# Experts of a routed layer in plain float32: two experts side by side in one block of 128 slots, a ring of 16 weight loads, results stored by token

## The chip, the cores and the metric

The kernel runs on one core of one Trainium2 chip, in one launch. The metric is the device time of that core in microseconds. The core has TensorE (PE: matmuls, with its weight loads shown as PEld), VectorE (DVE), ScalarE (ACT), GpSimd (POOL), a queue engine SyncE (SP) that issues most DMAs, and 16 DMA engines between the chip's main memory and the core's SBUF. The result of a matmul lands in PSUM. Each engine runs its own instruction list in order and waits for the others on semaphores.

## What is computed

Two layers (DEPTH 2) of a backbone on 256 context tokens and 512 latent tokens, width 1024, all in float32. Each layer has a token mixer (latent attention, neighbourhood attention, Fourier mixing, gates) and then routed experts. Layer 0 runs the experts for 768 tokens, layer 1 for the 512 latent ones. The change touches the experts alone:

```python
N_EXPERTS, TOP_K, D_MODEL, D_EXPERT = 32, 2, 1024, 512
def hier_moe(h, ...):
    p_grp = softmax(h @ w_rg + b_rg);  p_top, g_idx = top_k(p_grp, 1)        # 4 groups of 8
    e_in = (h @ w_re + b_re)[group g_idx];  l_top, e_loc = top_k(e_in, 2)
    w_tok = p_top * softmax(l_top);  e_ids = g_idx * 8 + e_loc
    for each token and each of its two experts e, weight w:
        out[token] += w * ((silu(x @ w_gate[e]) * (x @ w_up[e])) @ w_down[e])
```

w_gate and w_up are 1024x512 for each expert and w_down is 512x1024, 2 MiB each, 6.3 MB an expert and 201 MB a layer. With the reference's inputs the router gives these loads: in layer 0 the three fullest experts have 147, 139 and 99 tokens, the ninth fullest of experts 4 to 31 has 54, and experts 0 to 3 have 24, 35, 46 and 27. In layer 1 the fullest has 101, the ninth fullest of experts 4 to 31 has 45, and experts 0 to 3 have at most 15.

## The kernel before, in words

It is written for the five engines by hand: a function per engine, each a Python list of instructions, with semaphores between them (`then_inc`, `wait_ge`). Both layers are unrolled. Most tiles lie in one large SBUF tensor called `arena`, so a profile row reads `arena` for nearly all of them; `round` is the same memory seen as float32r, `slot`, `vbank` and `abank` are PSUM tiles, `xb` and the rest are slices of arena.

**Router.** For each tile of 128 tokens TensorE transposes the normalised rows (L807) and multiplies them with the router's weights (L813). SP stores the rows to `h_rows` in memory (L2247). VectorE then finds the group and the two experts of every token (L1375 to L1409). TensorE counts how many earlier tokens chose the same expert (L848, L851, L854), and from that a one-hot product gives for each expert the list of its tokens (L862, `ids`). `dest` says for each token and choice in which slot of `y_slots` its result will stand.

**Expert stage.** Each of the 32 experts has one block of 128 slots, in order of its number. POOL gathers the 128 rows of a block from `h_rows` by `ids` (L1998, two buffers `xb`). TensorE transposes them (XT, L890), does gate and up into `slot[0]`, transposes the product (AT, L918) and does down into `slot[1]` (L899 for all three). Weights come in units of 1 MiB, six for an expert (gate, gate, up, up, down, down). SP loads a unit into one of six raw buffers (L2269), in pieces of 2 KB, as soon as the unit that lay there has been split. ScalarE rounds it to float32r (`upper`, L1789), VectorE forms the difference (`lower`, L1458), both into a ring of four. Each product is then three products of float32r parts:

```python
for m, (st_, w) in enumerate(((ph, whi[n0 % RING]), (ph, wlo[n0 % RING]), (pl, whi[n0 % RING]))):
    last = pe.matmul(out_ap, st_, w[:, k, :], ...)        # L897 to L899
```

ScalarE copies the result of a block (L1811) and issues its store to `y_slots` (L1813), all 128 rows of it. One turn of the hardware loop does two experts (12 units). The down part of a block runs one block late, after gate and up of the next one.

**Start of the stage.** SP issues four units after the last row store and after the output projection's last matmul. A barrier of all five engines follows (L355); then the other units, the first transposes and the writing of the slot lists (L2013) begin.

**Extra blocks.** An expert with over 128 tokens gets more blocks, decided at run time: `ctl` holds their number and their experts, and each engine runs `extra_block` under a branch, 11 of them (NX), in plain float32 (L962, L969, L974, L980), with weights loaded whole (L2303 to L2309). Two of them run in layer 0 and none in layer 1. SP issues list and weights of the first one when all units have been split; POOL gathers its rows (L2028), ACT stores its result (L1862).

**End of the stage.** After a barrier POOL gathers for each token tile the two result rows by `dest` (L2044), TensorE mixes them with the token's two weights (L1000), and VectorE adds, normalises and goes on to the next layer or to the output. Slots of extra blocks that nobody writes are zeroed once at the start (L2127).

## Time and profile before

| | us |
|---|---|
| time, median of 3 runs | 3227.08 (3225.95 to 3227.56) |
| time of the profiled execution | 3230.56 |
| its span, first to last instruction | 3228.8 |
| TensorE busy | 2897.7 (90%) |
| VectorE busy | 1861.6 (58%) |
| ScalarE busy | 1401.7 (43%) |
| GpSimd busy | 420.4 (13%) |
| first expert matmul to the end of the last, layer 0 | 1049.9 to 1655.6 |
| the same, layer 1 | 2562.1 to 3166.8 |
| moved by DMA | 665.18 MB, mean 206 GB/s |

The profile is of one execution. Its span is 1.8 us shorter than that execution's own time, and that time lies 3.5 us above the median. Busy time of an engine is the union of its instructions; a busy engine need not be the one that the others wait for, which the chain of waits tells: it goes back from the last instruction to what released it. PE is matmuls, PEld the loads of the stationary operand that run beside them. A plain float32 matmul leaves two records, a float32r one leaves one. The clock is TensorE's granted clock as a share of 2.4 GHz. A row of a line in a helper function stands for all its callers.

### The profile page before, as it was taken

Reading aid. Unit: us, or ns where it says so; the run is one execution under the profiler, and the core shown is the slowest. Engines: PE = TensorE matmul, PEld = TensorE weight load, DVE = VectorE, ACT = ScalarE, POOL = GpSimd, SP = SyncE. Lnnn points to the kernel's source line nnn. Section 1 sums busy time; section 2 is a strip of 40 time slices with the busy share of each in tenths; the row PEclk is TensorE's granted clock in tenths of the full one; section 3 lists DMA queues with packets and bytes.
Section 4 is the critical chain, followed back from the end, with each engine's and each line's share of the span. In section 5 each row is a group of like instructions: output and inputs, shape, how many; then the busy total and the mean of one; then the engine's idle time right before and its main releaser. Section 6 shows DMA issues by size and latency. Waiting matters only on the chain.

```text
span 3228.8 us, 37959 instructions
## 1 busy us (share of the span) xinstructions
PE 2897.7 (90%) x13895; PEld 2091.6 (65%) x13895; DVE 1861.6 (58%) x2243; ACT 1401.7 (43%) x1710; POOL 420.4 (13%) x403
## 2 busy tenths in 40 slices
PE   5999898999995999999986699898999599999994
PEld 3655566788844787777752355466885488777772
DVE  3223566422247788888834413456334688888884
ACT  2200346422101677777730210346320377777770
POOL 1220000001112211111002310000011201111102
PEclk7999999999996999999988799999999699999997
DMA  9740002222143999999983550003333599999993
GB/s 303 245 156 26 6 1 36 69 69 59 46 139 113 349 393 392 392 393 392 392 318 150 172 164 26 6 2 75 97 104 120 182 379 392 392 392 392 392 392 122
DMA packets 400599, 665.18 MB, mean 206 GB/s; under 512 B 63744, under 2 KB 139920, under 8 KB 400096
## 3 DMA queue, kind: packets, MB, share of 16 engines
q1 hardware_dynamic: 365154, 541.75, 48.7%
q0 software_dynamic: 25824, 87.22, 7.6%
q10 hardware_dynamic: 9504, 34.61, 2.6%
q8 instruction: 79, 1.29, 0.2%
q14 instruction: 38, 0.31, 0.0%
HBM read 612.95 MB, written 53.39 MB: 206 GB/s over the span
## 4 chain that ended last, share of the span: by engine, by line
PE 52%; DMA 23%; DVE 11%; ACT 9%; issue 3%; SPq 1%; DVEq 0%; POOL 0%; PEldq 0%; ACTq 0%; POOLq 0%
DMA arena<-in_w_gate_e 22%; PE abank L771 11%; PE abank L559 7%; PE slot L899 7%; PE vbank L771 5%; PE slot L827 4%; DVE round L1458 4%; ACT round L1789 3%; PE vbank L612 3%; PE vbank L597 2%; PE vbank L696 2%; DVE nmx L1204 1%; PE vbank L528 1%; ACT arena L1603 1%; PE abank L584 1%
## 5 line engine op out<-in xcount | busy, mean ns | idle before, releaser
L899 PE MATMUL slot<-round,round 128*128 128x512 f32 x4608 | 1107.5, 397 | 62.3 <-DVE round L1466 57.5
L899 PEld LDWEIGHTS slot<-round,round 128*128 128x128 f32 x4608 | 860.2, 190 | 259.6 <-issue 54.3
L1458 DVE TENSOR_TENSOR round<-arena,round 128x2048 fp32r<-128x2048 f32 x384 | 872.5, 2287 | 161.0 <-ACT round L1789 160.7
L1789 ACT CAST round<-arena 128x2048 fp32r<-128x2048 f32 x384 | 734.5, 1915 | 327.0 <-DMA arena<-in_w_down_e 92.2
L771 PE MATMUL abank<-round,round 128*128 128x512 f32 (+1 forms) x1152 | 324.3, 360 | 8.3 <-DVE round L1279 8.3
L1998 POOL DMA_INDIRECT arena<-h_rows,ids x64 | 141.7, 2214 | 970.5 <-PE vbank L890 919.1
L771 PEld LDWEIGHTS abank<-round,round 128*128 128x128 f32 x1152 | 207.5, 190 | 43.2 <-issue 8.7
L559 PE MATMUL abank<-arena 128*128 128x512 f32 (+1 forms) x640 | 229.1, 517 | 3.3 <-ACT arena L1603 3.3
L1305 DVE TENSOR_TENSOR arena<-vbank,arena 128x512 f32<-128x512 f32 x72 | 43.4, 602 | 310.6 <-PE vbank L771 310.6
L771 PE MATMUL abank<-hT_low,round 128*128 128x512 f32 (+1 forms) x576 | 207.3, 360 | 0.0
L559 PEld LDWEIGHTS abank<-arena 128*128 128x128 f32 x640 | 121.9, 193 | 114.8 <-issue 102.9
L771 PE MATMUL vbank<-round,round 128*128 128x512 f32 (+1 forms) x864 | 178.2, 355 | 0.0
L1761 ACT ACTIVATE arena<-abank,bT 128x512 f32<-128x512 f32 x72 | 44.5, 618 | 290.5 <-PE abank L771 290.5
L771 PEld LDWEIGHTS vbank<-round,round 128*128 128x128 f32 x864 | 144.3, 189 | 24.3
L827 PE MATMUL slot<-arena 128*128 128x512 f32 x320 | 138.4, 593 | 3.4 <-POOL arena L1983 3.4
L1072 DVE SCALAR_TENSOR_TENSOR arena<-vbank,arena 2x512 f32<-2x512 f32 x20 | 13.6, 679 | 215.3 <-PE vbank L528 215.3
L1983 POOL TENSOR_TENSOR arena<-arena 128x512 f32<-128x512 f32 (+1 forms) x48 | 53.1, 1106 | 609.6 <-DVE arena L1305 609.6
L1616 ACT ACTIVATE arena<-abank,bT 128x512 f32<-128x512 f32 (+3 forms) x48 | 25.3, 543 | 231.8 <-PE abank L559 231.8
L771 PEld LDWEIGHTS abank<-hT_low,round 128*128 128x128 f32 x576 | 109.5, 190 | 17.0
L1279 DVE TENSOR_TENSOR round<-arena,round 128x1536 fp32r<-128x1536 f32 x48 | 89.2, 1858 | 52.6 <-ACT round L1728 52.6
L827 PEld LDWEIGHTS slot<-arena 128*128 128x128 f32 x320 | 60.5, 190 | 78.7 <-issue 74.6
L1662 ACT ACTIVATE arena<-slot,nmx 128x768 f32<-128x768 f32 (+1 forms) x80 | 65.2, 815 | 100.3 <-DVE nmx L1204 100.0
(248 smaller groups left out, 3402.2 us busy)
## 6 DMA issues: line engine op xcount, KB each, us to landing
arena<-in_w_gate_e SPq DMA_DIRECT2D x128, 1024.0 KB, 14.1
arena<-in_w_up_e SPq DMA_DIRECT2D x128, 1024.0 KB, 12.5
arena<-in_w_down_e SPq DMA_DIRECT2D x128, 1024.0 KB, 14.2
arena<-in_w_ada POOLq DMA_DIRECT2D x80, 512.0 KB, 5.0
y_slots<-arena ACTq DMA_DIRECT2D x66, 512.0 KB, 6.4
arena<-in_w_in SPq DMA_DIRECT2D x48, 512.0 KB, 4.2
arena<-in_w_in SPq DMA_DIRECT2D x8, 2048.0 KB, 12.6
arena<-in_w_ada SPq DMA_DIRECT2D x4, 2048.0 KB, 15.2
```

The costliest lines, as they stand in the source:

```text
L559: last = pe.matmul(ps[:, 0:nn], w[:, k, m * P:(m + 1) * P], hT[:, k, o:o + nn], start=(k == 0), stop=(k == KD - 1))
L597: last = pe.matmul(ps[:, 0:384], hT[:, k, t * P:(t + 1) * P], w[:, k, 0:384], start=(k == 0), stop=(k == KD - 1))
L612: last = pe.matmul(ps[:, 0:512], hT[:, k, t * P:(t + 1) * P], w[:, k, :], start=(k == 0), stop=(k == KD - 1))
L696: last = pe.matmul(ps[64 * e:64 * e + 64, 0:P], v[:, k, h * 64:(h + 1) * 64], PT[(i + e) % 4][:, k, :], start=(k == 0), stop=(k == kt - 1))
L771: last = pe.matmul(ps[:, 0:n], x, y, start=(k == 0 and q == 0), stop=(k == len(terms) - 1 and q == 2))
L827: last = pe.matmul(s[:, half * 512:(half + 1) * 512], mT[:, k, t * P:(t + 1) * P], w, start=(k == 0), stop=(k == KD - 1))
L899: last = pe.matmul(out_ap, st_, w[:, k, :], start=(first and k == 0 and m == 0), stop=(final and k == 3 and m == 2))
L1279: dve.tensor_tensor(glo[u % 2], graw[u % GRAW], ghi[u % 2].bitcast(F32), ALU.subtract).then_inc(glo_ready, 1)
L1458: dve.tensor_tensor(wlo[n0 % RING][:, :, :], raw[n0 % RAW][:, :, :], whi[n0 % RING][:, :, :].bitcast(F32), ALU.subtract).then_inc(lo_ready, 1)
L1662: act.activation(PR[i % 2][:, 0:nk], slot[(ib + i) % 2][:, 0:nk], ACT.Exp, bias=nmx[:, k:k + 1], scale=1.0, accum_out=rsum[:, k:k + 1]).th ...
L1789: act.copy(whi[n0 % RING][:, :, :], raw[n0 % RAW][:, :, :]).then_inc(hi_ready, 1)
L1998: pool.indirect_dma_start(out=xb[i % 2], out_offset=None, in_=h_d[:, :], in_offset=bass.IndirectOffsetOnAxis(ap=ids[:, i:i + 1], axis=0)). ...
```

## The change

- **Plain float32.** The splits into float32r parts go, on ScalarE and VectorE, for weights, rows and the middle. TensorE multiplies the loaded units themselves, one product where there were three.
- **Blocks of two experts.** A layer has 20 blocks of 128 slots instead of 32 (NB). Experts 0 to 3 stand in two fixed pairs. The other 28 are ranked by their number of tokens: the eight fullest have a block alone, the next 20 are paired. In a pair, slots 0 to 63 belong to one expert and 64 to 127 to the other: a product has a stationary operand of 128x64 and writes half of the partitions of a PSUM tile, and the two experts' products alternate. The order is the two fixed pairs, two ranked pairs, then eight times a single block and a pair.
- **Ranking.** VectorE and TensorE work out rank, block, half and capacity (128 alone, 64 in a pair) of each expert. The two fixed pairs' lists (`ids`, first two columns) are made first, the ranked ones while blocks 0 and 1 run. SP reads the ranked expert numbers from `eord` (a value load before the first unit of each) and addresses the weights with them.
- **Loads.** The ring has 16 units of 1 MiB, released by the matmuls themselves (`unit_used`). A unit's rows are dealt so that each partition reads 8 KB in one piece: four rows of gate or up, two whole rows of half the down matrix. xT and aT are taken in the matching order by a strided view. Four units are issued ahead of the row stores, ten behind them, two after the router's last transposes.
- **Rows and results by token.** `h_rows` holds every row twice (SP stores each tile twice), for first and second choice. A list names rows 0 to 1535, or 4096 for an empty slot, which a bounds check leaves out of gather and store. Results go by the same list to `y_rows` (POOL, an indirect store per block), so at the end SP loads them as plain tiles. `y_slots`, its zeroing and `dest` for whole blocks go.
- **Extra blocks** hold only what exceeds 128 or 64 slots; 15 may be needed. SP issues list and weights of the first one after the last unit has been used. POOL does gather, store and the wait for its landing, one block after the other.
- **Barriers** within and around the stage go, except those between the layers' phases elsewhere.

```diff
-RAW, RING = 6, 4
-UNITS = 6 * NE
+FIXED, HOT = 4, 8
+RANKED = NE - FIXED
+NB = FIXED // 2 + HOT + (RANKED - HOT) // 2
+NX = (2 * TOK - HOT * (P // 2 + 1)) // (P // 2)
+RAW = 16
...
+    order = pairs + cold[:spare]
+    for h, c in zip(hot, cold[spare:]):
+        order += [h, c]
...
+                def gate_or_up(i, part):
...
+                    for half in range(2):
+                        tiles = weights(i, part, half)
+                        for j in range(4):
+                            for at, w in tiles:
+                                last = pe.matmul(to[at, :], xT[i % 2][:, 4 * half + j, at], w[:, j, :],
+                                                 start=(half == 0 and j == 0), stop=(half == 1 and j == 3))
+                        release(last, i, part, half)
+                        if part == "gate" and half == 0 and i:
+                            middle_turned(i - 1)
...
+                rows_turned(0)
+                for i in range(NB):
+                    gate_or_up(i, "gate")
+                    gate_or_up(i, "up")
+                    if i + 1 < NB:
+                        rows_turned(i + 1)
+                    if i == 0:
+                        ranked_ids()
+                    else:
+                        down(i - 1)
+                middle_turned(NB - 1)
+                down(NB - 1)
...
-                    dst = raw[n0 % RAW]
-                        src = wdf[bass.ds(i * FE + (L * NE - 1) * FE, FE), (c - 4) * 512:(c - 3) * 512]
-                    sp.dma_start(dst, src.rearrange("(k p) f -> p k f", p=P)).then_inc(raw_in[n0 % RAW], 16)
+                        sp.dma_start(raw[n % RAW], src.rearrange("(p j) f -> p j f", j=4)).then_inc(raw_in[n % RAW], 16)
...
                 def extra_block(j, b, it):
                     with pool.If(count > j):
...
+                        pool.wait_ge(X["dve"], j * 3 + 3)
+                        pool.sem_inc(X["go"], 1)
+                        pool.indirect_dma_start(
+                            out=y_d[:, :], out_offset=bass.IndirectOffsetOnAxis(ap=idx_x[:, b:b + 1], axis=0),
+                            in_=yb[0], in_offset=None,
+                            bounds_check=2 * TOK - 1, oob_is_err=False).then_inc(X["y"], 16)
+                        pool.wait_ge(X["y"], j * 16 + 16)
+                        pool.sem_inc(X["y_out"], 1)
...
+                        if isinstance(j, int):
+                            sp.wait_ge(unit_used, mark["unit_used", L, len(units) - 1])
+                        else:
+                            sp.wait_ge(X["y_out"], j * 1)
```

What the change does to the instruction lists, at three places. Names with numbers (`round_4_62`) are single float32r views, the shape is the output's, `x16` counts instructions alike.

TensorE inside the first gate part of layer 0, before: two slices k of one unit.

```order
L899 MATMUL slot<-round_4_62,round_8_70 128x512
L899 MATMUL slot<-round_4_66,round_8_70 128x512
L899 MATMUL slot<-round_4_62,round_8_72 128x512
L899 MATMUL slot<-round_4_63,round_8_70 128x512
L899 MATMUL slot<-round_4_67,round_8_70 128x512
L899 MATMUL slot<-round_4_63,round_8_72 128x512
```

TensorE after, around the first block of a single expert (L993 gate and up, L1010 down, L966 and L976 transposes):

```order
L993 MATMUL slot<-arena 64x512 x24
L966 MATMUL vbank<-cst,arena 128x128 x4
L966 MATMUL abank<-cst,arena 128x128 x4
L1010 MATMUL slot<-arena 64x512 x16
L993 MATMUL slot<-arena 128x512 x4
L976 MATMUL abank<-cst,arena 128x128 x4
L993 MATMUL slot<-arena 128x512 x12
```

Where 24 products of three kinds stood for a unit pair's worth of weights there are 8 for one expert and 16 of 64 partitions for two; the down part of the pair before stands between the transposes and the next gate part.

SP at the start of layer 0's stage, before, from the last router bias on:

```order
L2069 DMA arena<-in_b_re 128x32
L2247 DMA h_rows<-arena 128x1024 [waits hrow_ready] x6
L2269 DMA arena<-in_w_gate_e 128x4x512 [waits groups_done]
L2269 DMA arena<-in_w_gate_e 128x4x512
L2269 DMA arena<-in_w_up_e 128x4x512 x2
L2269 DMA arena<-in_w_gate_e 128x4x512 [waits h_out1,h_out0,phase_act,phase_pool,phase_dve,phase_pe]
L2269 DMA arena<-in_w_gate_e 128x4x512
L2269 DMA arena<-in_w_up_e 128x4x512 [waits lo_ready] x2
```

SP after, from the last row store on (the four units of w_gate_e that now stand ahead of the twelve row stores are left out):

```order
L2316 DMA h_rows<-arena 128x1024 [waits hrow_ready]
L2316 DMA h_rows<-arena 128x1024
L2309 DMA arena<-in_w_up_e 128x2048 [waits groups_done]
L2309 DMA arena<-in_w_up_e 128x2048 x3
L2309 DMA arena<-in_w_gate_e 128x2048 x4
L2309 DMA arena<-in_w_up_e 128x2048 x2
L2309 DMA arena<-in_w_up_e 128x2048 [waits h_out1,h_out0,groups_done]
L2309 DMA arena<-in_w_up_e 128x2048
L2304 DMA arena<-in_w_down_e 128x2048 [waits unit_used,expert_order]
```

Ten units stand behind the row stores with no wait for another engine's phase, where four stood, and the first wait for a used unit comes at the 17th.

POOL at the end of layer 0's stage, before:

```order
L1998 DMA arena<-h_rows,ids 128x1024 [waits xt_done] x30
L2019 TENSOR_LOAD ctl
L2019 ISA x2
L2022 COMPARE_AND_BRANCH [waits xt_done]
L2028 DMA arena<-h_rows,idx_x 128x1024 [waits x0_ids0]
L2022 UNCONDITIONAL_BRANCH
L2036 MEMSET arena 128x128 [waits phase_act,phase_sp,phase_dve,phase_pe]
```

POOL after, from the last result stores to the first extra block:

```order
L2034 DMA y_rows<-arena,ids 1536x1024 [waits y_ready] x5
L2065 TENSOR_LOAD ctl [waits y_stored0,y_stored1,vec_taken]
L2065 ISA x2
L2067 MEMSET arena 128x128
L2070 COMPARE_AND_BRANCH
L2076 DMA arena<-h_rows,idx_x 128x1024 [waits x0_ids0]
L2082 DMA y_rows<-arena,idx_x 1536x1024 [waits x0_dve]
L2070 UNCONDITIONAL_BRANCH [waits x0_y]
```

The first extra gather now stands behind the wait for all result stores, and each extra block has its store, and the wait for it, ahead of the next block's gather.

## Rows read from the trace of the kernel before

**Rows 1.** The page's line of GB/s, 40 slices of 80.7 us each.

```profile
GB/s 303 245 156 26 6 1 36 69 69 59 46 139 113 349 393 392 392 393 392 392 318 150 172 164 26 6 2 75 97 104 120 182 379 392 392 392 392 392 392 122
```

**Rows 2.** Stretches: us, busy of PE, PEld, DVE, ACT, POOL, clock, DMA, GB/s.

```profile
1000.00:1050.00 50.00, 23.06 (x113) 21.10 (x111) 33.21 (x77) 12.21 (x13) 10.35 (x8) 0.50 0.48 167
...
1042.00:1656.00 614.00, 582.73 (x2688) 474.62 (x2688) 522.78 (x350) 453.07 (x351) 89.34 (x43) 0.98 1.02 377
2554.00:3167.00 613.00, 581.02 (x2688) 474.68 (x2688) 522.73 (x351) 452.94 (x351) 76.41 (x38) 0.98 1.01 374
```

**Rows 3.** Chain of waits, layer 0: start us, us, engine, tile, line, count.

```profile
1138.82 14.06 DMA arena<-in_w_gate_e
...
1648.20 7.36 PE slot L899 x24
...
1667.56 16.31 PE slot L969 x32
...
1699.85 14.02 PE slot L969 x32
...
1717.32 10.16 PE slot L980 x16
...
1744.37 5.14 PE slot L1000 x8
```

**Rows 4.** DMA queues from 1200 to 1400 us: packets, MB, share of 16 engines.

```profile
q1 hardware_dynamic: 33858, 67.25, 90.7%
q10 hardware_dynamic: 1584, 5.77, 7.1%
q0 software_dynamic: 1506, 5.45, 7.0%
```

**Rows 5.** DMA packets from 2457 to 2465 us, before the expert stage of layer 1.

```profile
DMA packets 894, 3.26 MB, mean 407 GB/s; under 512 B 102, under 2 KB 102, under 8 KB 893
```

**Rows 6.** Chain of waits, dense stretches of TensorE (the columns of rows 3).

```profile
893.96 55.20 PE slot L827 x128
...
1083.88 0.87 PE vbank L890 x8
1084.76 10.93 PE slot L899 x48
```

**Rows 7.** Timeline of PE: start us, us, engine, line, operation, shapes, count.

```profile
162.65 1.90 PE L528 MATMUL vbank<-arena,csT 128*2 128x512 f32 x16
164.48 10.59 PE L559 MATMUL abank<-arena 128*128 128x512 f32 x32
...
401.61 1.53 PE L696 MATMUL vbank<-arena 128*64 128x128 f32 x24 [0.50 <-ACT arena L1674]
```

**Rows 8.** Timeline where the two stages begin, the columns of rows 7.

```profile
1007.55 1.39 SPq L2269 DMA_DIRECT2D arena<-in_w_gate_e  x2
...
1033.02 1.12 POOL L1998 DMA_INDIRECT arena<-h_rows,ids  x1 [27.24 <-DVE ids L1430]
...
1042.10 0.93 SPq L2269 DMA_DIRECT2D arena<-in_w_gate_e  x2
...
1049.89 10.35 PE L899 MATMUL slot<-round,round 128*128 128x512 f32 x35 [5.84 <-DVE round L1466]
...
2545.61 1.11 POOL L1998 DMA_INDIRECT arena<-h_rows,ids  x1 [22.62 <-DVE ids L1430]
...
2562.07 13.24 PE L899 MATMUL slot<-round,round 128*128 128x512 f32 x48 [5.90 <-DVE round L1466]
```

**Rows 9.** DMA issues of the whole run: count, KB each, us to landing.

```profile
y_slots<-arena ACTq DMA_DIRECT2D x66, 512.0 KB, 6.4
...
arena<-h_rows,ids POOLq DMA_INDIRECT x64, 8.6
```

**Rows 10.** Timeline at the end of layer 1's stage, the columns of rows 7.

```profile
3159.43 7.38 PE L899 MATMUL slot<-round,round 128*128 128x512 f32 x24 [2.40 <-DVE round L1471]
...
3189.89 16.58 PE L1000 MATMUL slot<-arena 128*128 128x512 f32 x32 [23.07 <-DMA arena<-y_slots,dest]
```

More of the change, by code:

```diff
@@ L903, in gate_or_up @@
-                def gate_or_up(n0, it, b, which):
-                    for kh in range(2):
-                        parts = [(xTh[b][:, 4 * kh + k, :], xTl[b][:, 4 * kh + k, :]) for k in range(4)]
-                        unit(n0 + kh, it, parts, slot[0][:, which * FE:(which + 1) * FE], kh == 0, kh == 1)
-                def GU_wait(b, i):
-                    pe.wait_ge(xl_ready, i * 2 + (2 * EB + 2))
-                    if not (isinstance(i, int) and EB + i <= 0):
-                        pe.wait_ge(amid, i + EB)
@@ L2275, in _ @@
+                sp.wait_ge(groups_done, mark["h8_used", L, len(qtiles(L)) - 1])
                 for b in range(2):
[L2276 to L2285 removed]
```

716 lines of the change are left out of this document (369 added, 347 removed).

## The prediction, made before the changed kernel was run

> **What bounds the kernel now.** I read the slices of the page first. Of 40 slices the 15th to the 20th and the 34th to the 39th stand at 392 to 393 GB/s [rows 1]: these are the two expert stages. The stretches say the same: 614 us in layer 0 and 613 us in layer 1, with TensorE busy 583 and 581 us of them at a granted clock of 0.98 [rows 2]. Two engines look full, so the chain of waits has to decide. In both stages it steps through a DMA of w_gate_e per expert, 25 times in layer 0 (the first stands in [rows 3]) and 24 times in layer 1. So DMA is the bound, and TensorE is just behind it. The other 2000 us (attention, gates, router) are nearly untouched by the change and I carry them over.
>
> What fills the DMA engines: in 200 us of the stage 78.5 MB move, of which 67.3 MB are weights in pieces of 2 KB, 5.8 MB stores of results and 5.5 MB gathers of rows [rows 4]. The shares of the three queues divide these into 371, 406 and 389 MB per ms of engine time, so the 4 KB pieces are moved 5 to 9% faster than the 2 KB ones. A stretch in layer 1 that loads almost only 4 KB pieces runs at 407 GB/s [rows 5].
>
> **TensorE's work.** One plain float32 product of 128x512 appears as two records: 128 records take 55.20 us, so a product takes 0.8625 us. The split form takes three products at 10.93/48 = 0.228 us, 0.683 us together [rows 6]. Plain float32 therefore costs TensorE 26% more for one expert alone: 24 x 0.8625 = 20.7 us, plus 8 transposes at 0.87 and 4 more at half of that, is 22.0 us [rows 6], against 16.4 + 1.3 before. What pays for it is the pair, if both halves of 64 columns run side by side. They do so in two rows of before: the 12 products of L696 (stationary 128x64, two column halves in turn, 128 moving columns) take 1.53 us for 24 records where 24 x 0.431/4 = 2.59 would be needed one after the other; and 8 products of 512 columns in four column groups take 1.83 us to the start of the next instruction, where 8 x 0.8625 = 6.9 would be serial and 1.73 is a perfect overlap [rows 7]. I take the pair as overlapped: a block of two experts costs 22.0 us, like a block of one. 20 blocks are 440 us a layer, 22.0 us on average, against 32 x 17.7 = 566 before.
>
> The same row of L528 prices the change between tilings: 1.83 - 1.73 = 0.1 us for going in and out [rows 7]. The Trainium skill, page TensorEngine Tiling (Array Packing), section Key Properties, says that changing the tiling mode drains TensorE, which speaks against putting transposes and whole blocks between halves. With some five changes in a block it would be worth 5 x 0.05 x 20 = 5 us a layer by the row; it lies in cover of the DMA.
>
> VectorE and ScalarE lose the splits of weights. They don't end the waits of the steady part, the DMAs do, so this alone gives nothing there.
>
> **DMA's work after.** The weights stay: 192 loads of 1.0486 MB a layer. Rows are gathered and results stored for real assignments only, unused slots being out of bounds: 1536 x 4 KB x 2 = 12.6 MB in layer 0 and 8.4 MB in layer 1, instead of 16 + 16 MB. That no time is spent on skipped rows is not seen in any row; if each slot cost full, 20 x 0.52 x 2 = 21 MB would move, 20 and 31 us more. I take the skip. The rate: pieces of 8 KB have no row; below stands 392 [rows 1], the nearest is 407 at 4 KB [rows 5], and the same step upward again is 423. I take 407.
>
> There is less to load after the start. Before, 4 loads are issued at 1007.6, the others wait for a barrier at 1042.1 [rows 8]. After, 4 go ahead of the h rows (the queue is idle then), 10 follow the last h row, 2 the end of the router's transposes: from 1007.6 on 12 x 2.58 = 31 us, so the 16 are in by 1039. Ids for the four fixed experts are made at the same place (before: 1033.0, POOL's first gather [rows 8]). The added ranking stands behind them on VectorE and TensorE and lies in the 8.6 us that a gather takes to land [rows 9]; it is over before 1042, or costs what it is late. First transpose 1042, first expert product 1045 (before 1049.9). TensorE stands at 1.2 GHz then [rows 2], so the first quarter takes 4 x 1.725 = 6.9 us and loads resume at 1052.
>
> From there DMA moves 176 x 1.0486 + 12.6 = 197.1 MB, at 407 484 us. TensorE needs 4 + 440 us for the same, so the ring (16 loads, 41 us) is never full again and drains only slowly: four pair blocks take 12 loads per 22 us where 8.5 arrive, leaving about 3 of 16, then a whole block (6) and a pair (12) take 18 per 44 us where 17 arrive. End: 1052 + 484 + 5 (landing, the last 4 products of 0.86, run-out) = 1541, before 1655.6 [rows 3]: **-114 us**. If DMA cost nothing TensorE would end at 1045 + 4 + 440 + 3 = 1492, so the cover is 49 us a layer.
>
> Layer 1: first gather at 2545.6, first product at 2562.1 [rows 8]. After, by the same steps: 2545.6 + 8.6 + 3 = 2557, resume 2564, 184.6 + 8.4 = 192.9 MB, 474 us, end 3043 against 3166.8 [rows 10]: **-124 us**.
>
> **The ends of the stages.** Layer 0 has two extra blocks, after as before (147 and 139 tokens; ranks above eight have at most 54). Before, the first starts 12.0 us after the last L899 and the second 2.5 us after the first one's last product [rows 3], since their lists, weights and rows had come ahead. After, the list and weights are asked for only when the last unit has been used, and POOL gathers only once the last result has landed: copy 1.0, issue 1.2, landing 6.4 [rows 9], gather 0.9 + 6, transposes 2, copies 1.3, some 20 us (+9). Between the two, POOL waits for the first extra's store to land before it reaches the next gather: 1.2 + 1.2 + 3 + 0.9 + 3 + 1 + 1.3 = 12 (+10). Queued behind that wait are the gather and so TensorE. At the end the barrier and the twelve gathers (16.9 us from L980's end to L1000) give way to one store and plain loads: 1.2 + 1.2 + 3 + 0.5 + 4.6 = 10.5 (-6). Together **+13 us**, from 0 to +30. Layer 1 has none of these, so its 23.1 us [rows 10] become 1.0 + 1.2 + 4 + 0.5 + 4.6: **-12 us**. 15 tested branches instead of 11 run beside the last store. The second store of each h row goes to an idle queue beside the router (113 GB/s in that slice [rows 1]), and the zeroing of y_slots lay beside attention: both at nothing; if the cover fails, 6 x 2 us.
>
> **Sum.** -114 - 124 + 13 - 12 = -237. The profiled execution took 3230.6 (span 3228.8), so 2994 on its terms; the median was 3227.1, so **2990**.
>
> **The rivals.**
> *Larger pieces give nothing* (0.20). The 392 may be set beyond the engines. For it: it is flat to 0.3% over 400 us [rows 1]. Against: the 407. At 392 the stages take 503 + 492: 37 us more, 3027. The Trainium skill, page DMA: Bandwidth & Descriptors, section Where 436 GB/s comes from, puts the limit of a load from HBM on the HBM side, at about 358 GB/s a core; the trace is above that figure, but a limit of that kind is this rival.
> *TensorE becomes the bound* (0.15). When the ring has run down, a pair's quarter is 3.45 us of work per 5.2 us of loading; if the granted clock falls to 1.2 GHz in these gaps, or halves overlap only in part, a pair costs about 28 us: 12 x 28 + 8 x 22 = 512, ends 1564 and 3076: 56 us more, 3046. It decides from 24.2 us for a mean block. For it: the clock of 0.50 (1.2 GHz) between 1000 and 1050 us, where TensorE is half idle [rows 2]. Against: 0.98 over the stages, where it is 95% busy.
> *The column halves run one after the other* (0.05): the other side. A pair is then 41.4 + 1.3 = 42.7 us, the stage 12 x 42.7 + 8 x 22 = 688; ends 1740 and 3252, 85 and 86 us later than before, with +13 - 12: 3399. It is slower from 35 us a pair on. L696 and L528 speak against it; for it only that no row has 64 columns with 512 moving ones.
> The remaining 0.05 are stalls of POOL's in-order queue (gather and store of a row list share it) that empty xb or yb: 3100.
>
> **How the numbers follow.** Forecast 0.55, at 2990, its own range 2950 (423 GB/s: 36 less) to 3020 (extras +30, some stalls). The range 2940 to 3070 takes in the first two rivals and a mix of them. About 0.2% is what a measurement of this kernel can tell from no change. Faster 0.94, within 0.2% 0.01, slower 0.05.
>
> **What would show it.** Right: 16 products of 64x512 per pair's down part in about 7.1 us; a chain that steps through weight loads, stages at 400 GB/s or more from about 1052 to 1540; VectorE busy under 15% there; L993's idle time ended by DMA. Wrong: GB/s at 392 (first rival), TensorE's busy share at 98% with DMA under 9 (second), 14 us for those 16 products (third). Gaps of over 15 us at 1541 or between the extra blocks would make the ends mis-sized.

## The result and the profile of the changed kernel

The changed kernel takes 2981.4 us (median of 4 runs, 2980.6 to 2986.0) against 3227.3 us (3226.0 to 3232.5) of the kernel before: ratio 0.9238, 95% interval 0.9222 to 0.9254, 246 us less. The forecast was 2990, the range 2940 to 3070. The profiled execution took 2980.6 us with a span of 2978.7, so span against span 250.1 us went. The same views as before, now of the changed kernel. The page's line of GB/s, 40 slices of 74.5 us:

```profile
GB/s 291 184 201 39 6 1 6 64 65 64 64 39 221 233 361 421 422 420 421 420 349 65 217 184 104 0 6 12 87 93 108 193 229 413 421 421 420 419 416 181
```

Where [rows 1] has 392 there is 421, and both plateaus are shorter. Stretches (us, busy of PE, PEld, DVE, ACT, POOL, clock, DMA, GB/s), which answer to [rows 2]:

```profile
1045.00:1533.00 488.00, 459.47 (x1802) 190.77 (x1802) 45.55 (x88) 55.00 (x79) 49.14 (x49) 0.99 0.98 407
2447.00:2931.00 484.00, 458.57 (x1794) 189.74 (x1791) 44.51 (x84) 54.81 (x79) 45.23 (x45) 0.99 0.98 403
1200.00:1400.00 200.00, 187.35 (x697) 79.58 (x697) 17.19 (x26) 22.82 (x33) 17.15 (x17) 0.99 1.01 421
1040.00:1045.00 5.00, 2.08 (x10) 1.71 (x12) 1.32 (x2) 0.76 (x2) 0.00 (x0) 0.50 0.30 116
1045.00:1050.00 5.00, 5.00 (x14) 1.62 (x16) 0.00 (x0) 1.10 (x1) 0.00 (x0) 0.57 0.01 3
```

VectorE's 523 us of each stage are 45 now. TensorE is still busy for 94% of it and DMA for all of the steady part, so again the waits must say who is the bound. The waits from 1100 to 1520 us (total, times, longest):

```profile
PE slot L993 <- DMA arena<-in_w_up_e: 24.3, 14, 2.5
PE slot L993 <- DMA arena<-in_w_gate_e: 2.8, 2, 2.0
PE slot L1010 <- DMA arena<-in_w_down_e: 0.4, 1, 0.4
```

Before it was VectorE's splits, L1466, that TensorE waited for directly and DMA behind them; now TensorE waits for weights themselves, 27 us in 420. DMA is the bound, by 7%. A pair and a single block in the timeline of PE (start us, us, engine, line, shapes, count, idle before):

```profile
1202.03 7.09 PE L1010 MATMUL slot<-arena 128*64 128x512 f32 x32
1208.94 3.60 PE L993 MATMUL slot<-arena 128*64 128x512 f32 x16
1212.48 0.74 PE L976 MATMUL abank<-cst,arena 128*128 128x128 f32 x4
1213.15 3.65 PE L993 MATMUL slot<-arena 128*64 128x512 f32 x16
1219.27 8.78 PE L993 MATMUL slot<-arena 128*64 128x512 f32 x32 [2.46 <-DMA arena<-in_w_up_e]
...
1229.05 7.03 PE L1010 MATMUL slot<-arena 128*128 128x512 f32 x16
...
1239.81 10.47 PE L993 MATMUL slot<-arena 128*128 128x512 f32 x24
```

The down part of a pair, 16 products of 64 columns (32 records), takes 7.09 us; that of one expert, 8 products of 128 columns, 7.03. Two experts cost TensorE the time of one, but for half a microsecond a block (e6). The ends of the stage in layer 0, same columns (the first three lines are POOL's, PE's and SP's at the start; [rows 8] and [rows 3] stand against them):

```profile
1033.75 1.18 POOL L2026 DMA_INDIRECT arena<-h_rows,ids  x1 [28.74 <-DVE rk L1517]
...
1044.90 16.12 PE L993 MATMUL slot<-arena 128*64 128x512 f32 x64 [0.72 <-issue]
...
1050.81 4.18 SPq L2304 DMA_DIRECT2D arena<-in_w_down_e  x4
...
1513.68 3.65 PE L993 MATMUL slot<-arena 128*64 128x512 f32 x16 [1.52 <-DMA arena<-in_w_up_e]
...
1525.99 7.09 PE L1010 MATMUL slot<-arena 128*64 128x512 f32 x32 [1.12 <-ACT arena L1863]
1551.84 1.97 PE L1040 MATMUL vbank<-cst,arena 128*128 128x128 f32 x8 [18.76 <-DMA arena<-h_rows,idx_x]
1555.19 17.02 PE L1047 MATMUL slot<-arena 128*128 128x512 f32 x32 [1.38 <-DVE arena L1603]
...
1598.52 15.84 PE L1047 MATMUL slot<-arena 128*128 128x512 f32 x32 [1.38 <-DVE arena L1603]
...
1634.77 5.74 PE L1075 MATMUL slot<-arena 128*128 128x512 f32 x7 [9.80 <-DMA arena<-y_rows]
```

And layer 1, with its last lines against [rows 10]:

```profile
2446.72 16.64 PE L993 MATMUL slot<-arena 128*64 128x512 f32 x64 [0.72 <-issue]
...
2911.82 3.65 PE L993 MATMUL slot<-arena 128*64 128x512 f32 x16 [1.35 <-DMA arena<-in_w_up_e]
...
2940.72 4.71 PE L1075 MATMUL slot<-arena 128*128 128x512 f32 x7 [9.51 <-DMA arena<-y_rows]
```

So the 250.1 us fall apart like this: the last down product of layer 0 ends at 1533.1 instead of 1655.6 (-122.5); from it to the combination 101.7 us instead of 88.8 (+12.9); from there to the first gather of layer 1 801.2 us in both; from that gather to the last down product of layer 1 495.2 us instead of 621.2 (-126.0); the tail before the last combination 9.5 us instead of 23.1 (-13.6); the rest -0.9.

### The profile page after: what moved, and what is told of

Read it like the earlier page. It is cut to its first block and busy times, and to the rows that moved or that the text cites. A ratio compares the mean times of both kernels' runs of the same rounds, so it can differ in the third digit from the quotient of the medians.

```text
span 2978.7 us, 31492 instructions
## 1 busy us (share of the span) xinstructions
PE 2655.2 (89%) x12155; PEld 1527.5 (51%) x12155; DVE 900.1 (30%) x1711; ACT 600.4 (20%) x1166; POOL 334.8 (11%) x400
## 5 line engine op out<-in xcount | busy, mean ns | idle before, releaser
L993 PE MATMUL slot<-arena 128*64 128x512 f32 (+1 forms) x2048 | 578.4, 603 | 52.8 <-DMA arena<-in_w_up_e 47.0
L993 PEld LDWEIGHTS slot<-arena 128*64 128x64 f32 (+1 forms) x2048 | 212.6, 152 | 382.6 <-issue 377.9
L1010 PE MATMUL slot<-arena 128*64 128x512 f32 (+1 forms) x1024 | 283.0, 595 | 2.6 <-ACT arena L1863 2.2
L812 PEld LDWEIGHTS abank<-round,round 128*128 128x128 f32 x1152 | 206.7, 190 | 42.7 <-issue 8.7
L1585 DVE TENSOR_TENSOR arena<-slot,arena 128x512 f32<-128x512 f32 x40 | 27.7, 692 | 566.0 <-ACT arena L1878 566.0
L1010 PEld LDWEIGHTS slot<-arena 128*64 128x64 f32 (+1 forms) x1024 | 100.7, 150 | 156.9 <-issue 151.6
L812 PEld LDWEIGHTS vbank<-round,round 128*128 128x128 f32 x864 | 144.1, 188 | 24.2
L1588 DVE TENSOR_TENSOR arena<-slot,arena 128x512 f32<-128x512 f32 x40 | 27.7, 692 | 281.2 <-PE slot L993 281.2
L2026 POOL DMA_INDIRECT arena<-h_rows,ids x40 | 41.4, 1034 | 578.0 <-PE abank L966 454.8
L703 PE MATMUL slot<-arena 96*128 96x256 f32 (+1 forms) x288 | 102.5, 475 | 3.5 <-ACT arena L1729 1.8
```

The costliest lines, as they stand in the source:

```text
L703: last = pe.matmul(s[:, o:o + nn], qT[h % 2][0:QK, t * P:(t + 1) * P], kT[h % 4][0:QK, o:o + nn], start=True, stop=True)
L812: last = pe.matmul(ps[:, 0:n], x, y, start=(k == 0 and q == 0), stop=(k == len(terms) - 1 and q == 2))
L993: last = pe.matmul(to[at, :], xT[i % 2][:, 4 * half + j, at], w[:, j, :], start=(half == 0 and j == 0), stop=(half == 1 and j == 3))
L1010: last = pe.matmul(slot[1][at, hf * 512:(hf + 1) * 512], aT[i % 2][:, 2 * half + j, at], w[:, 2 * j + hf, :], start=(half == 0 and j == 0) ...
L2026: pool.indirect_dma_start(out=xb[i % 2], out_offset=None, in_=h_d[:, :], in_offset=bass.IndirectOffsetOnAxis(ap=ids[:, at:at + 1], axis=0) ...
```

## The experiments

All are edits of the changed kernel. "Stage" is the time from the first product on L993 to the end of the last on L1010 (up to 4 lines lower in some of these kernels), in layer 0 and layer 1. The stretch between the two stages, from the combination of layer 0 to the first product of layer 1, came out at 808 to 817 us in these kernels (811.9 in the changed one), though hardly an edit bears on it. So two totals can differ by a few us from what their stages give. In e6 the kernel computes with half of the weights.

| run | edit | us | ratio to before, 95% | stages, us |
|---|---|---|---|---|
| changed kernel | | 2981.4 | 0.9222 to 0.9254 | 488.2, 484.5 |
| e1 | 2 KB pieces, down 4 KB | 3033.1 | 0.9373 to 0.9402 | 515.3, 510.9 |
| e2 | 4 KB pieces | 3005.9 | 0.9288 to 0.9316 | 500.1, 495.3 |
| e3 | ring of 8 | 3015.0 | 0.9325 to 0.9353 | 509.0, 505.0 |
| e4 | extra blocks prepared ahead | 2954.8 | 0.9137 to 0.9162 | 487.8, 484.2 |
| e5 | runs of four products a half | 3017.3 | 0.9327 to 0.9364 | 504.9, 503.2 |
| e6 | half of the weights loaded | 2913.7 | 0.9007 to 0.9043 | 455.0, 454.2 |
| e7 | all pairs first | 3060.4 | 0.9460 to 0.9498 | 527.3, 521.1 |
| e8 | no row skipped in gathers | 2995.1 | 0.9260 to 0.9291 | 492.4, 489.5 |
| e9 | runs of eight products a half | 3221.4 | 0.9973 to 0.9994 | 606.2, 604.7 |
| e10 | three loads held back | 2974.6 | 0.9210 to 0.9238 | 487.8, 483.2 |
| e11 | e4 and e10 together | 2949.0 | 0.9125 to 0.9157 | 488.3, 483.8 |

### Is it the piece or the depth of the queue? (e1, e2, e3)

Two things changed in the loads at once: pieces grew from 2 KB (and 4) to 8, and the ring from 6 to 16. In e1 the rows of a tile go back to their old places, and the transposes follow (e2 puts two rows side by side):

```diff
-x = xb[i % 2].rearrange("p (h q j) -> p h j q", h=2, j=4)
+x = xb[i % 2].rearrange("p (h j q) -> p h j q", h=2, j=4)
-sp.dma_start(raw[n % RAW], src.rearrange("(p j) f -> p j f", j=4))
+sp.dma_start(raw[n % RAW], src.rearrange("(j p) f -> p j f", j=4))
```

> The changed kernel with one part undone: the loads of the gate and up weights in pieces of 2 KB and those of the down weights in pieces of 4 KB, as before the change; ring, order, tiling and everything else stay. Theory (the size of the pieces sets the rate, 421 GB/s at 8 KB against 392 at 2 KB with some 4 KB ones among them): some 196 MB per stage from 1051 us on take 500 us instead of 466, so each of the two stages is 33 us longer, GB/s stands at 390 to 396 in it, and the kernel takes 2981 + 66 = 3047 us. Rival (the deeper ring, with 16 loads in flight instead of 6, gave the rate): 418 GB/s or more and 2981 within 6 us.

> As the run with 2 KB pieces, but all weights of the ring in pieces of 4 KB. If the rate follows the piece (407 GB/s in the one stretch of 4 KB pieces before the change), a stage takes 16 us more and the kernel 2981 + 32 = 3013 us. If 8 KB gives nothing over 4 KB, 2981. If the ring's depth set the rate, also 2981, and then the run with 2 KB stands there too.

DMA packets from 1200 to 1400 us, e1, then e2:

```profile
DMA packets 33574, 78.86 MB, mean 394 GB/s; under 512 B 2163, under 2 KB 2163, under 8 KB 33568
```

```profile
DMA packets 22205, 81.83 MB, mean 409 GB/s; under 512 B 2247, under 2 KB 2247, under 8 KB 22198
```

With 16 loads in flight all the same, the rate is 394, 409 and 421 GB/s. It follows the piece, and the rival of depth falls. So does another one, that the rate rose because less other traffic runs beside the loads: e1 has the gathers and stores of the changed kernel and still stands at 394, next to the 392 of before. The price is a little smaller than expected (27 and 26 us a stage instead of 33, 12 and 11 instead of 16): by the measured 394 and 409 the 196 MB of a stage would take 32 and 14 us more, so 1 to 2 us of the difference are the rate, and the remaining 2 to 6 us I can't place.

e3 makes the ring shorter and leaves the pieces:

```diff
-RAW = 16
-RAW_AT = (0, 1, 6, 7, 2, 3, 8, 9, 14, 15, 10, 11, 12, 13, 4, 5)
+RAW = 8
+RAW_AT = (0, 1, 6, 7, 2, 3, 4, 5)
```

> The changed kernel with a ring of 8 loads instead of 16, pieces still of 8 KB. Theory (DMA bounds the stage, its rate is that of the piece, and the depth counts only for what is loaded ahead of the first product): 8 loads fewer are in at the start of each stage, which is 8 x 2.5 = 20 us of loading that moves behind it, so 2981 + 40 = 3021 us, up to 3035 with some waits where a pair of experts empties the ring, and 415 to 421 GB/s in the stage's steady part. Rival (depth makes the rate): 392 GB/s and some 2981 + 66 + 40 = 3087 us. Rival (neither matters, TensorE is the bound): 2981.

```profile
DMA packets 13119, 83.49 MB, mean 417 GB/s; under 512 B 2278, under 2 KB 2278, under 8 KB 3590
```

417 GB/s at half the depth: the depth of the ring is worth its 8 loads at the start, 20.8 and 20.5 us a stage where 20 were expected. But layer 0 ended only 14.4 us later, because its first product came at 1038.5 instead of 1044.9. 3.0 of these 6.4 us are an earlier issue of the first gather (1030.7 instead of 1033.8), the rest is its shorter landing. That was not expected, and led to e10.

### How far is TensorE behind? (e6)

```diff
-sp.dma_start(raw[n % RAW], src.rearrange("(p j) f -> p j f", j=4))
+sp.dma_start(raw[n % RAW][:, 0:2, :], src.rearrange("(p j) f -> p j f", j=4)[:, 0:2, :])
-last = pe.matmul(to[at, :], xT[i % 2][:, 4 * half + j, at], w[:, j, :],
+last = pe.matmul(to[at, :], xT[i % 2][:, 4 * half + j, at], w[:, j % 2, :],
```

> The changed kernel with half of the DMA's work in the ring taken away: only the first half of each weight tile is loaded, in pieces of 4 KB, and each product that would read the second half reads the first again (this computes with half of the weights). TensorE's work is unchanged. Theory (DMA bounds the stage, TensorE is 28 us behind it by its idle time that weight loads ended): the stage ends when TensorE's work does, at 1045 + 4 + 20 x 22 + some run-out, a stage of 455 to 460 us instead of 488 and 484, and the kernel takes 2981 - 56 = 2925 us. If TensorE were the bound already: 2981, within 6 us.

Its stages as stretches, columns as above:

```profile
1041.00:1496.00 455.00, 453.71 (x1802) 186.88 (x1802) 45.66 (x89) 54.35 (x79) 49.08 (x49) 1.00 0.71 234
2409.00:2864.00 455.00, 452.96 (x1794) 186.01 (x1794) 45.11 (x86) 55.48 (x80) 45.15 (x45) 0.99 0.69 226
```

TensorE is busy throughout and DMA for 70%, and a stage takes 455 us: 33 and 30 less than in the changed kernel. That is all that a faster DMA could still bring inside the stages. The total fell by 68 us where 56 were expected: the stages give 63.5 of them, where the waits for weights had suggested 28 in each, and the first product of layer 0 came 3.7 us earlier. A block of one expert takes 22.1 us there (from the down part at 1212.91 to the next at 1235.03), as forecast to 0.1, a pair 22.6 (1190.27 to 1212.91).

### Does the order of the blocks matter? (e7)

```diff
-    order = pairs + cold[:spare]
-    for h, c in zip(hot, cold[spare:]):
-        order += [h, c]
-    return order
+    return pairs + cold + hot
```

> The changed kernel with the blocks in another order: all twelve blocks of two experts first, then the eight of one expert, where the changed kernel lets them alternate from the fifth block on. Theory (a ring can even out only 16 loads): the twelve pairs are bound by their 144 loads, of which 128 come after the start, 128 x 2.49 + some 15 for rows = 334 us, and TensorE waits in them; the eight single blocks after them are bound by TensorE, 8 x 22 = 176 us. The stage ends at 1051 + 334 + 3 + 176 = 1564 to 1567 instead of 1533, and the kernel takes 2981 + 68 = 3049 us. Rival (DMA moves the same bytes, so the order changes nothing): 2981.

```profile
1100.00:1380.00 280.00, 227.25 (x1000) 85.72 (x998) 21.66 (x41) 25.62 (x37) 18.99 (x19) 0.96 1.01 421
1400.00:1560.00 160.00, 160.00 (x450) 75.61 (x449) 14.54 (x22) 19.47 (x28) 12.02 (x12) 1.00 0.80 325
```

The same bytes and the same products take 39 and 37 us more a stage, where 34 were expected. In the first stretch DMA is full and TensorE idle for 53 of 280 us, in the second TensorE is full and DMA has room. Two resources at 94% and 100% need an order that keeps both at work; the ring can carry 16 loads from one block to the next, and twelve pairs want more.

### What do the column halves need to overlap? (e5, e9)

```diff
-                        for j in range(4):
-                            for at, w in tiles:
+                        for at, w in tiles:
+                            for j in range(4):
```

> The changed kernel with the products of a pair in another order: within each part all products of the one expert (columns 0 to 63), then all of the other (columns 64 to 127), where the changed kernel alternates. The same products with the same operands. Theory (two halves overlap only where they are neighbours in the order): the last product of one run overlaps the first of the next, so 8 products take 6 x 0.8625 us instead of 4 x 0.8625, a pair 31 + 1.3 = 32.4 us instead of 22, a stage 12 x 32.4 + 8 x 22 = 565 us instead of 486, and the kernel some 3140 us. With no overlap at all: 43 us a pair, 688 us a stage, 3383 us. If TensorE finds the other half whatever the order: 2981 us. The 16 products of a pair's down part take 10.4, 13.8 or 7.1 us in these cases.

Timeline of PE, e5, a pair's three quarters after its transposes, and a pair's down part:

```profile
1099.28 12.51 PE L993 MATMUL slot<-arena 128*64 128x512 f32 x48
...
1139.60 8.97 PE L1010 MATMUL slot<-arena 128*64 128x512 f32 x32
```

Alternating, these take 10.5 (e6, the same 48 records) and 7.1 us; one after the other they would take 20.7 and 13.8. So all three of my cases were wrong: halves that aren't neighbours overlap too. In the first stretch of a like block the other half's first product starts at 1227.49, 1.8 us after 1225.71, when two of the four products that stand ahead of it have started; so two products run alone at the start of a stretch and two at its end, which costs 2 us each time. A pair takes 26.6 us (1212.60 to 1239.22), TensorE is busy in 400 of 400 us, and it has become the bound: a stage takes 17 and 19 us more. The next run asks how far this reaches, with all eight products of one expert's part ahead of the other's eight:

> The run in which four products of one expert stood ahead of four of the other took 12.5 us for three quarters of a pair where 10.4 are a perfect overlap, and 3017 us in all: halves overlap even when they aren't neighbours. Here the same with runs of eight: in each part all eight products of the one expert's two loads, then all eight of the other's. Theory (TensorE lets a product on the free columns start while at most some two products, four records, of the other half stand waiting ahead of it): a run of four hides in steady state behind that, a run of eight doesn't, and a part of 16 products takes 10.5 to 11.6 us instead of 7, a pair 33 to 36 us, a stage 12 x 34.5 + 8 x 22.3 = 592 us instead of 486, and the kernel some 3190 us. Rival (it looks ahead as far as is wanted, and only the first run of a part stands alone): 24 to 26 us a pair, some 3017 us. If nothing overlapped: 3383 us.

```profile
1252.32 11.00 PE L1013 MATMUL slot<-arena 128*64 128x512 f32 x29
1262.73 0.64 PE L994 MATMUL slot<-arena 128*64 128x512 f32 x1
1263.15 0.59 PE L1013 MATMUL slot<-arena 128*64 128x512 f32 x1
...
1287.24 7.03 PE L1013 MATMUL slot<-arena 128*128 128x512 f32 x16
```

A pair takes 34.9 us here (1252.32 to 1287.24), and TensorE is busy in 500 of 500 us, so the later release of the weights in this order does not bear on it. The overlap reaches a few products ahead and no further, as the theory said, with 30 us of the total under-estimated. The lines also show it directly: near the end of the down part on L1013 products of the next part on L994 run between its last ones, on the half that has become free. At 34.9 us a pair the whole gain is gone but for 6 us (ratio 0.998), which is the break-even of 35 us that the prediction gave for its rival.

### Skipped rows (e8)

The gathers take a second list, in which a slot without a token names the row of its own number:

```diff
+link(dve.tensor_scalar(t, ps[:, 0:a1 - a0], 0.0, cst[:, C_TOKF:C_TOKF + 1], ALU.is_equal, ALU.mult))
+link(dve.tensor_tensor(t, t, ps[:, 0:a1 - a0], ALU.add))
+link(dve.tensor_scalar(gids[:, a0:a1], t, float(NONE), None, ALU.add))
-in_offset=bass.IndirectOffsetOnAxis(ap=ids[:, at:at + 1], axis=0),
+in_offset=bass.IndirectOffsetOnAxis(ap=gids[:, at:at + 1], axis=0),
```

> The changed kernel, but its gathers skip no row: a slot without a token, whose index was out of bounds, reads the token row of its own number (its result is still not stored). Layer 0 has 1054 such slots of 2560, layer 1 1536, so 4.3 and 6.3 MB more are moved. Theory (a skipped row costs nothing on the DMA engines, and they are the bound): at 421 GB/s 10 and 15 us more, 3006 us. Rival (a skipped row takes an engine as long as a moved one, so that only the bytes were spared): 2981. If TensorE were the bound: 2981 too, but then with 421 GB/s nowhere in the stage.

DMA from 1045 to 1533 us, the changed kernel, then e8:

```profile
DMA packets 31642, 198.59 MB, mean 407 GB/s; under 512 B 5744, under 2 KB 5744, under 8 KB 9092
...
q0 software_dynamic: 5712, 11.67, 6.3%
```

```profile
DMA packets 31332, 201.57 MB, mean 413 GB/s; under 512 B 4707, under 2 KB 4707, under 8 KB 8782
...
q0 software_dynamic: 5568, 15.23, 7.9%
```

The queue of the gathers moves 3.6 MB more and takes 1.6% of 488 us more, 8 us: full price for rows that are moved. This window leaves out the first two gathers and the last 5 us of e8's stage; from 1030 us to the end of either stage this queue has 6000 packets in both kernels, e8 has 1054 fewer under 512 B, which is the number of skipped slots, and 4.3 MB more. The packets show the cost directly: one of a skipped row has 4 bytes and takes 9.6 ns of an engine, a moved row 161 ns. So the skip saves DMA time, as the theory said.

The stages grew by only 4 and 5 us, though, where 10 and 15 were expected. In layer 0 the 3.7 MB that e8 moves more between the release of the first loads and the last load's landing are 8.8 us at 421 GB/s, but that stretch grew by 5.2 us (477.6 to 482.8). The missing 3.6 us stand in the mean rate, 418 GB/s instead of 415, and most of them in its last 15 us: 390 GB/s where the changed kernel has 309. Why the DMA engines are better filled there with all rows moved isn't shown, and for layer 1 it stays open.

### The start and the end of a stage (e4, e10, e11)

e4 loads the first extra block's list when the lists are written, its gate and up weights when their places in the ring are free, gathers its rows before the last two stores, and gathers the next block's rows ahead of the store of the one before:

```diff
+                with sp.If(count > 0):
+                    e = sp.value_load(ctl[0:1, 0:1], min_val=0, max_val=NE - 1)
+                    sp.dma_start(idx_x[:, 0:1], slot_d[L][0:P, :]).then_inc(X["ids0"], 16)
+                    for k, w, dst, r in (("wg0", wgf, wg[0], 1), ("wu0", wuf, wu[0], 5)):
+                        sp.wait_ge(unit_used, mark["unit_used", L, len(units) - RAW + r])
...
+                    if i == NB - 2:
+                        gather_first()
                     result(i)
...
+                    with pool.If(count > j + 1):
+                        pool.wait_ge(X["pe"], (j + 1) * 4 + 1)
+                        gather(1 - b, it + b)
                     with pool.If(count > j):
```

> The changed kernel with the extra blocks of layer 0 prepared ahead: the first one's list is loaded as soon as the lists are written, its gate and up weights as soon as their places in the ring are free, its rows are gathered ahead of the last two stores, and each further gather stands ahead of the store of the block before it on POOL instead of behind that store's landing. Theory (list, gather and landing lie on the path, and TensorE waits for them): from the last down product to the extra's first product 22.1 us become 4 to 5 (8 transposes and two copies), and the 12.7 us between the two blocks become 3: 27 us less, 2954 us. Rival (the weights, which queue behind the ring's last loads, arrive late): half of it, 2968. Rival (the early loads take DMA time from the ring's last units, and what is won is lost there): 2981.

```profile
1527.45 7.09 PE L1010 MATMUL slot<-arena 128*64 128x512 f32 x32 [1.12 <-ACT arena L1863]
1538.15 1.57 PE L1038 MATMUL vbank<-cst,arena 128*128 128x128 f32 x8 [3.62 <-DMA arena<-h_rows,idx_x]
1541.10 16.14 PE L1045 MATMUL slot<-arena 128*128 128x512 f32 x32 [1.38 <-DVE arena L1603]
...
1560.72 7.13 PE L1058 MATMUL slot<-arena 128*128 128x512 f32 x16 [0.67 <-ACT arena L1894]
1567.69 1.04 PE L1038 MATMUL vbank<-cst,arena 128*128 128x128 f32 x8
1570.37 14.00 PE L1045 MATMUL slot<-arena 128*128 128x512 f32 x32 [1.64 <-DVE arena L1603]
```

26.6 us less, as expected. From the last down product to the extra's first the 22.1 us are 6.6 (4 to 5 expected: the list's load had queued behind the ring's, and POOL got it at 1530.9, so the rows are still waited for), and the second block follows after 2.5 us instead of 12.7.

e10 holds the last three of the first 16 loads until the first rows are in:

```diff
-                for n in range(4, RAW - 2):
+                for n in range(4, RAW - 3):
...
-                for n in range(RAW - 2, RAW):
+                sp.wait_ge(rows_got[0], 16 * (NB // 2 * L + 1))
+                for n in range(RAW - 3, RAW):
                     load_unit(n)
```

> The changed kernel, but the last three of the ring's first 16 loads wait until the gather of the first block's rows has landed. In the changed kernel that gather stands at 1034 us beside loads that are queued until 1039, and takes 7.9 us to land where the run with a ring of 8 shows 4.2; then DMA is idle until 1051, when the first loads are released. Theory (the stage is bound by DMA from that moment on, so that an earlier first product is worth what DMA stands idle less): first product at 1040 to 1041 instead of 1045 in layer 0, 5 us less there and 1 us in layer 1, where loads are still queued at the gather; 2975 us. Rival (the held loads are missed in the first blocks): 2981 or a few us more.

```profile
1033.52 1.18 POOL L2026 DMA_INDIRECT arena<-h_rows,ids  x1 [28.75 <-DVE rk L1517]
...
1037.78 1.13 PE L966 MATMUL vbank<-cst,arena 128*128 128x128 f32 x4 [3.31 <-DMA arena<-h_rows,ids]
...
1041.29 15.81 PE L993 MATMUL slot<-arena 128*64 128x512 f32 x64 [1.52 <-DVE arena L1578]
...
1046.92 4.17 SPq L2304 DMA_DIRECT2D arena<-in_w_down_e  x4
```

The first gather is issued 0.2 us earlier (1033.52 against 1033.75) and its rows are in 4.4 us earlier (first transpose at 1037.78 against 1042.20), the first product comes 3.6 us and the release of the first loads 3.9 us earlier, and layer 0's stage ends 4 us earlier at the same length. In layer 1 the first product comes 8.9 us after the gather instead of 10.7. The total of 2974.6 us lies where the theory put it, but the interval of its ratio meets the changed kernel's: the times alone don't settle 7 us, the trace's 4 us in layer 0 are what shows it.

> The preparation of the extra blocks ahead (2954.8 us by itself) and the three held loads together. If the two are independent: 2955 - 6 = 2949 us. If the held loads bring nothing: 2955.

2949.0 us, ratio 0.9141 (0.9125 to 0.9157), the number expected. That is 32 us less than the changed kernel and faster than both kernels of this document; against e4 alone the 6 us are within the intervals, so this run doesn't show that the two gains add up.

## Why the prediction held, step by step

**The bound.** Right, and so were three of its signs: VectorE busy for 9% (under 15% named), DMA at 400 GB/s or more, L993's waits ended by DMA. The fourth, a chain that steps through weight loads, can't be read: the chain of the changed kernel's profile breaks off at 2933 us, behind both stages. DMA bounds both stages: TensorE's idle time in them is ended by weight loads, less DMA work (e6) shortens them by 30 to 33 us, and a lower rate (e1, e2) lengthens them.

**The rate of 8 KB pieces.** Mis-sized: 407 GB/s was taken, with 423 as the upper bound, and the steady part runs at 421. The step in the text that took the nearest row instead of following the trend of two rows (from 392 to 407) failed by 14 GB/s, 16 us a stage, and e1 and e2 put 394, 409 and 421 in its place. The trend also gives diminishing steps, 15 and 12. The first rival, that larger pieces give nothing, is out. The Trainium skill, page Perfetto Trace Analysis, section Roofline, puts the practical ceiling of a core that alone is active at some 120% of 358 GB/s, an estimate of about 430 by its figures; 421 fits that and not the 358 which the prediction weighed.

**The loading as a whole, and the end of a stage.** That error was hidden by another one, and that the two nearly cancelled was luck. The sum lets all bytes move at one rate, from the release of the first loads on, and ends the stage 5 us after the last load. With 421 GB/s these steps would have given 1525.2 in layer 0 and 481.6 us after the first gather in layer 1; it was 1533.1 and 495.2, not far from the forecast's 1541 and 497.

The 5 us were right: the last load has landed at 1528.4 and 2926.6, and the stage ends 4.7 us later in both layers. But TensorE's last wait for weights is for the last *up* weights (L993 at 1513.68, "<-DMA arena<-in_w_up_e"). Behind them stand 3.6 us of products, the down part of block 18, four transposes, a copy of ScalarE and the down part of block 19, 19.4 us in both layers, which no load shortens. The last six down loads, 14.8 us, lie beside them, and the last of these is in about 1 us before its products start.

What took longer is the loading: 477.6 and 473.4 us from the release to the last landing, where 421 GB/s would give 468.2 and 458.2. Of these 9.4 and 15.2 us, 2.3 and 4.1 are bytes that the sum didn't have (198.05 and 194.61 MB instead of 197.1 and 192.9; above all, SP already loads for the next part). 1.5 and 1.8 stand in the first 5 us, which run at 295 and 267 GB/s, 3.9 and 5.3 in the last 15, at 309 and 271 GB/s, and 1.7 and 4.1 between them, at 419 and 417 GB/s. Why the last 15 us are slower isn't shown. Layer 0, the columns of [rows 2]:

```profile
1050.80:1055.80 5.00, 5.00 (x26) 1.84 (x24) 0.69 (x1) 0.60 (x1) 0.00 (x0) 1.00 0.81 295
1055.80:1513.60 457.80, 430.48 (x1696) 179.93 (x1692) 44.17 (x86) 51.79 (x75) 48.17 (x48) 1.00 1.01 419
1513.60:1528.40 14.80, 13.59 (x48) 5.77 (x50) 0.69 (x1) 1.50 (x2) 0.97 (x1) 1.00 0.76 309
```

Over the whole loading this makes 413 and 407 GB/s for the bytes of the sum: the 407 that was meant for the steady part fits the mean. So 16 us too much for the steady part, 9 and 15 too little for the rest, and a start 1 us too late left 8 us in layer 0 (-122.5 against -114) and 2 in layer 1 (-126.0 against -124).

**TensorE's blocks.** Right but for 0.6 us: 22.0 us forecast for either kind, 22.1 measured for a single block and 22.6 for a pair (e6), 16 products of 64 columns in 7.09 us. TensorE's stage alone was put at 447 us and is 455; 3.6 of the 8 us are the lists of the ranked experts (L925, L931, L937) that now stand in the first blocks and had no term. The pairs' 0.5 us more, 12 times, are 6 us a layer. That is the size of the 5 us that the prediction had for the changes between tilings and left out of the sum as covered by the DMA; a pair's block has such changes and a single one's hasn't, but no run measures them apart from its other differences. The cover of 49 us a layer became 30 to 33. The second rival's limit stands: TensorE takes 455 us at a mean block of 22.4, so the 488 of the stage are reached at 22.4 + 33/20 = 24.1 us, the text's 24.2. e5 has 24.8 and e9 29.8, which by this count gives 503 and 603 us a stage (505 and 606 measured). The granted clock stood at 0.99 in the stages, so a fall of the clock, one of its two causes, did not come.

**The overlap of halves.** Right in its result, and the rival with its 3399 us was priced too high, since it took all or nothing. e5 and e9 show what lies between: 26.6 and 34.9 us a pair. The Trainium skill, page TensorEngine Tiling (Array Packing), section Key Properties, says that tiles operate independently and may load weights and multiply in parallel; e5 agrees, and e9 shows that with eight products of the other half ahead more than half of the overlap is gone (34.9 us a pair between 22.6 and the 42.7 without any).

**The start.** First product at 1044.9 (forecast 1045) and resumed loads at 1050.8 (1052); in layer 1 10.7 us from gather to product (11.6). The first quarter took 5.9 us instead of 6.9, as the granted clock rose (0.50 before it, 0.57 in its first 5 us, 1.00 behind). The 8.6 us for a gather's landing were copied from the kernel before as a price; it took 7.9 (median of the first two), and e3 and e10 show that about half of it is made by the loads queued beside it: 4.1 to 4.2 without them.

**Skipped rows.** Right: they cost next to nothing. A skipped row of a gather takes 9.6 ns of an engine instead of 161. The 20 and 31 us that the other bound put on them were too much; gathers alone, half of it, were worth 4 to 5 us a stage. Skipped rows of the result stores were not put to the test by a run.

**The extras and the tails.** +12.9 us against +13, from 22.1, 12.7 and 9.8 us against 20, 12 and 10.5; the tail of layer 1 -13.6 against -12. The terms written down for the first gap add up to 18.8, and 20 - 12.0 is 8, not the 9 in the sum. This was forecast from the order of the issues alone. Ahead of the first extra the link that counted is the landing of the last result stores: the list was in at 1535.1, the last store at 1542.4, and the gather went out at 1544.6. Between the two extras it is the store's landing too (1590.6, the gather at 1591.9). e4 takes both off the path and wins 15.5 and 10.2 us; the list would have been in time, and only in e4 does it become the one that is waited for.

## What to carry to other kernels

When a stage runs at the DMA's rate, the size of the contiguous piece is a lever of its own; choosing which rows share a partition cost nothing here, since a transpose follows that can undo it. Then look at both edges of the stage: what is queued beside the transfer that starts it, which load the end really waits for, and how far the rate falls there; the rate of the steady part is not the mean of the stage (421 against 415 and 411 GB/s up to the last load). And when two resources are nearly balanced, order and granularity decide as much as the totals: the same work took 37 us more a stage with the heavy blocks in front.

## What was not expected of the hardware

- The DMA engines, with weight loads of 1 MB from one queue for the most part, ran at 394, 409 and 421 GB/s with pieces of 2 (and 4), 4 and 8 KB, at one and the same depth; with 8 loads in flight instead of 16, 417.
- Products on the two column halves overlap when four of one stand ahead of four of the other, and a product starts before some that stand ahead of it: 12.5 us for what takes 10.5 alternating and 20.7 serially. With runs of eight a pair takes 34.9 us instead of 22.6.
- The first two gathers (59 and 73 rows of 4 KB, the other slots skipped) landed after 7.9 us beside queued loads and after 4.1 to 4.2 us with no load queued.
- A row skipped as out of bounds appears as a packet of 4 bytes and takes 9.6 ns of an engine, a moved row of 4 KB 161 ns.
